# Decoder layer on Trainium2: the first weight slice in two quarters, and VectorE makes the first memory slice's high part

## What is computed

```python
h = rmsnorm(x, norm_g)
z = h @ w_in                                   # 2048 x 7168
...
mem_h = rmsnorm(mem, mem_norm_g)
mk, mv = jnp.split(mem_h @ w_mem_kv, 2, axis=-1)   # 2048 x 1024: keys, values
y_m = memory_attention(q_m, mk, mv) * jax.nn.silu(g_m)
...
y = jnp.concatenate([y_a, y_p, y_m], axis=-1) @ w_out
return rmsnorm(x + y, final_norm_g)
```

## Time and profile before

| what | us |
|---|---|
| median of 3 runs | 440.05 (439.99 to 440.51) |
| the profiled execution, its own time | 439.82 |
| span of its instructions | 437.6 |
| TensorE busy | 428.5 |
| VectorE busy | 266.3 |
| ScalarE busy | 220.1 |

### The profile page before, as it was taken

The page is one execution under the profiler, slowest core; times in us unless marked ns, Lnnn a source line. Parts: engine busy times, 40 slices in busy tenths (PEclk is TensorE's granted clock), DMA queues, the critical chain, the costliest instruction groups (busy, mean ns, idle before and its releaser), DMA issues.

```text
span 437.6 us, 6006 instructions
## 1 busy us (share of the span) xinstructions
PE 428.5 (98%) x2252; PEld 367.8 (84%) x2252; DVE 266.3 (61%) x293; ACT 220.1 (50%) x298; POOL 26.5 (6%) x48
## 2 busy tenths in 40 slices
PE   9999999999999999999999999999999999999992
PEld 8888888888888888888988888888888888888881
DVE  4865865545464685746466767848663674648522
ACT  6854784743444435536545444454465544357311
POOL 1000000000000020000020200010000202020200
PEclk9999999999999999999999999999999999999998
DMA  8999969655556554643629866445735256746022
GB/s 286 405 402 411 389 197 381 193 187 183 190 176 193 188 169 161 189 145 99 194 97 355 318 202 199 160 168 185 219 119 192 95 175 212 228 156 194 0 97 97
DMA packets 25657, 89.77 MB, mean 205 GB/s; under 512 B 2976, under 2 KB 3232, under 8 KB 24736
## 3 DMA queue, kind: packets, MB, share of 16 engines
q1 hardware_dynamic: 24336, 81.69, 54.9%
q10 hardware_dynamic: 1296, 7.73, 4.3%
HBM read 87.31 MB, written 2.10 MB: 204 GB/s over the span
## 4 chain that ended last, share of the span: by engine, by line
PE 95%; issue 2%; DVE 0%; POOL 0%; ACT 0%; POOLq 0%; DVEq 0%
PE ps L365 38%; PE ps L368 17%; PE ps L387 11%; PE ps L389 11%; PE ps L388 11%; PE ps L374 1%; PE ps L444 1%; PE ps L404 1%; PE ps L435 1%; PE ps L431 1%; PE ps L399 1%; PE ps L419 1%; PE ps L403 0%; PE ps L436 0%; PE ps L415 0%
## 5 line engine op out<-in xcount | busy, mean ns | idle before, releaser
L699 DVE TENSOR_TENSOR w_lo<-w_raw,w_hi 128x1024 fp32r<-128x1024 f32 x137 | 173.9, 1282 | 119.4 <-ACT w_hi L524 119.0
L524 ACT ACTIVATE w_hi<-w_raw 128x1024 fp32r<-128x1024 f32 x137 | 143.7, 1058 | 130.1 <-PE ps L368 74.6
L365 PE MATMUL ps<-xT,w_hi 128*128 128x512 f32 x640 | 200.6, 397 | 0.0
L368 PEld LDWEIGHTS ps<-xT,w_lo 128*128 128x128 f32 x600 | 112.7, 188 | 26.6
L368 PE MATMUL ps<-xT,w_lo 128*128 128x256 f32 x600 | 118.1, 278 | 0.0
L365 PEld LDWEIGHTS ps<-xT,w_hi 128*128 128x128 f32 x640 | 98.8, 189 | 1.3
L387 PE MATMUL ps<-w_hi,yT 128*128 128x512 f32 x112 | 43.6, 389 | 0.0
L388 PE MATMUL ps<-w_lo,yT 128*128 128x512 f32 x112 | 43.6, 389 | 0.0
L389 PE MATMUL ps<-w_hi,yT 128*128 128x512 f32 x112 | 43.6, 389 | 0.0
L387 PE MATMUL ps<-w_hi,xT 128*128 128x512 f32 x64 | 25.5, 399 | 0.0
L389 PE MATMUL ps<-w_hi,xT 128*128 128x512 f32 x64 | 25.0, 390 | 0.0
(11 more groups left out here) (129 smaller groups left out, 384.9 us busy)
## 6 DMA issues: line engine op xcount, KB each, us to landing
w_raw<-in_w_in SPq DMA_DIRECT2D x96, 512.0 KB, 4.2
w_raw<-in_w_out SPq DMA_DIRECT2D x32, 512.0 KB, 4.2
w_raw<-in_w_mem_kv SPq DMA_DIRECT2D x13, 512.0 KB, 13.1
x_t_raw<-in_x_t SPq DMA_DIRECT2D x8, 256.0 KB, 13.6
rows<-in_x ACTq DMA_DIRECT2D x2, 1024.0 KB, 10.5
rows<-in_mem ACTq DMA_DIRECT2D x2, 1024.0 KB, 9.0
x_res<-in_x ACTq DMA_DIRECT2D x2, 1024.0 KB, 8.9
mem_raw<-in_mem_head SPq DMA_DIRECT2D x3, 512.0 KB, 7.6
```

The costliest lines, as they stand in the source:

```text
L365: pe.matmul(ps[:, bank0(g) + f, :], hi[:, t, f * P:(f + 1) * P], moving[:, kt], start=(kt == 0), stop=(kt == KT - 1), skip_group_check=True)
L368: m = pe.matmul(ps[:, bank0(g) + f, 0:S], lo[:, t, f * P:(f + 1) * P], moving[:, kt, 0], start=False, stop=(kt == KT - 1), skip_group_chec ...
L524: act.activation(halves_of(n)[0], w_raw[:, n % RAW], ACT.Copy).then_inc(hi_done, 1)
L699: dve.tensor_tensor(lo, w_raw[:, n % RAW], hi.bitcast(F32), ALU.subtract).then_inc(lo_done, 1)
```

## The change

ScalarE issues weight slice (0, t=0) as two DMAs of 256 columns each (two quarters of a piece) and makes the high part of each quarter when it has landed. VectorE, not ScalarE, makes the high part of memory slice 0, as soon as the slice has landed; its waits for the table and for the constants stand behind its work on the first three pieces. TensorE runs 8 products of ones instead of 10. A new function `first_slice` does the t = 0 half of piece 0 in twelve matmuls of 256 columns: high x high (two features after each quarter), then high weights x low memory slice, then low weights x high memory slice.

```diff
+        quarter_landed = [sem(f"quarter_landed{i}") for i in range(2)]
+        quarter_hi = sem("quarter_hi")
+        mem_first_hi = sem("mem_first_hi")
...
+            def first_slice():
+
+                hi, lo = halves_of(0)
+                for f in range(NF):
+                    if f % 2 == 0:
+                        pe.wait_ge(quarter_hi, f // 2 + 1)
+                    pe.matmul(ps[:, bank0(MK) + f, 0:S], hi[:, 0, f * P:(f + 1) * P], memT[:, 0, 0],
+                              start=True, stop=False, skip_group_check=True)
+                pe.wait_ge(mem_lo, 1)
+                for f in range(NF):
+                    pe.matmul(ps[:, bank0(MK) + f, S:], hi[:, 0, f * P:(f + 1) * P], memT[:, 0, 1],
+                              start=False, stop=False, skip_group_check=True)
+                pe.wait_ge(first_lo, 1)
+                for f in range(NF):
+                    pe.matmul(ps[:, bank0(MK) + f, 0:S], lo[:, 0, f * P:(f + 1) * P], memT[:, 0, 0],
+                              start=False, stop=False, skip_group_check=True)
...
-                for t in range(TPP):
+                for t in range(int(n == 0), TPP):
...
-                    if n == 0 and t == 0:
-                        pe.wait_ge(first_lo, 1)
...
-            keep_warm(10, 7)
+            keep_warm(8, 7)
+            pe.wait_ge(mem_first_hi, 1)
+            first_slice()
...
-                    pe.wait_ge(mem_lo, TPP * (a + 1) if a >= HALVED else TPP * a + 1)
+                    if n:
+                        pe.wait_ge(mem_lo, TPP * (a + 1) if a >= HALVED else TPP * a + 1)
...
-                if n == 0:
-                    pe.wait_ge(first_hi, 1)
-                elif n < HALVED:
+                if 0 < n < HALVED:
                     pe.wait_ge(first_lo, n + 1)
...
-                if t == 0:
+                if n == 0 and t == 0:
+                    for q in range(2):
+                        c = slice(q * COLS // 2, (q + 1) * COLS // 2)
+                        act.wait_ge(quarter_landed[q], 16)
+                        act.activation(w_hi[:, 0, 0, c], w_raw[:, 0, 0, c], ACT.Copy).then_inc(quarter_hi, 1)
+                elif t == 0:
...
-            act.dma_start(w_raw[:, 0, 0], kv_dram[0, 0, :, 0]).then_inc(first_landed[0], 16)
+            for q in range(2):
+                c = slice(q * COLS // 2, (q + 1) * COLS // 2)
+                act.dma_start(w_raw[:, 0, 0, c], kv_dram[0, 0, :, 0, c]).then_inc(quarter_landed[q], 16)
...
-                    mem_to_hi((TPP * n + t,))
+                    if n or t:
+                        mem_to_hi((TPP * n + t,))
...
-                    dve.wait_ge(first_hi, n + 1)
+                    if n == 0:
+                        dve.wait_ge(quarter_hi, 2)
+                    else:
+                        dve.wait_ge(first_hi, n)
...
-                    dve.wait_ge(mem_hi, kt + 1)
+                    if kt:
+                        dve.wait_ge(mem_hi, kt)
+                    else:
+                        dve.wait_ge(mem_first_hi, 1)
...
-            dve.wait_ge(table_loaded, 1)
-            dve.wait_ge(consts_ready, 3)
+            dve.wait_ge(mem_first_landed, 16)
+            dve.tensor_scalar(memT[:, 0, 0], mem_t(0), mem_raw[:, 0:1], None, ALU.mult).then_inc(mem_first_hi, 1)
...
+            dve.wait_ge(table_loaded, 1)
+            dve.wait_ge(consts_ready, 3)
```

More of the change, by code:

```diff
@@ L467, in _ @@
                     pe.wait_ge(y_lo, min(a // 2 + 1, len(GATES)))
-                if n == 0:
-                    pe.wait_ge(first_hi, 1)
-                elif n < HALVED:
+                if 0 < n < HALVED:
                     pe.wait_ge(first_lo, n + 1)
-                else:
+                elif n:
                     pe.wait_ge(lo_done, n + 1)
@@ L544, in mem_to_hi @@
                 for kt in kts:
-                    if kt == 0:
+                    if kt == 1:
                         act.wait_ge(mem_first_landed, 16)
-                    elif kt in MEM_CHUNKS:
+                    if kt in MEM_CHUNKS:
                         act.wait_ge(mem_landed[MEM_CHUNKS.index(kt)], 16)
```

## The result

The changed kernel takes 442.69 us (median of 6, 441.0 to 443.48) against 440.05: **slower by 0.54%**, ratio 1.0054, 95% interval 1.0044 to 1.0064 (the two medians themselves stand 0.60% apart). The forecast was 440.4 in a range up to 441.3. The profiled execution took 441.66, with a span of 439.6, 2.0 us more than before. Note the spread: 2.5 us over six executions, where the kernel before has 0.5.

The account below looks back on a forecast made before the run. TensorE's unbroken stream behind piece 4, gated by a DMA landing, was taken as the bound. A second half 0.8 us late, less 0.41 absorbed, gave piece 4 0.4 us later: 440.4 us for the median, range 439.5 to 441.3.

Parts of the forecast that it names:

- The head start: Start of piece 0: fewer warm-up matmuls, VectorE's scaling and quarter copies let TensorE start at about 4.57, 0.76 us sooner.
- What the split moves in the queue: ScalarE's DMA queue: 128 more packets ahead put memory slice 1 back from 5.42 to at most 6.45, taken as about 6.25.
- nothing is paid: ScalarE's start: one DMA more takes 0.45 us and pushes the table load, which ends before anything has landed.
- The second half: Piece 0, t = 1: 1.76 us from slice landing to low weights, start at 8.1, 0.8 us late, at most 0.95.
- the point of 1.29 us: Delay and clock together beyond which the kernel counts as slower: 0.41 us of pauses plus 0.88 us of measuring tolerance.
- The absorption of 0.41 us: Ahead of pieces 3 and 4: TensorE's pauses of 0.18 and 0.23 us vanish and take up that much delay.
- piece 4's gate: Start of piece 4: the chain from its weights' DMA landing stays at 17.49, since the bytes ahead are the same.
- The clock: Rival, early TensorE work: new pauses make the clock rise later, costing 1.0 to 1.5 us more, 441.4 to 441.9; chance 0.17.
- the two rivals: Start of the kernel: clock rising later, chance 0.17, and memory slice landing later still, about 441.1, chance 0.06.
- Absorbed whole: Rival, first DMA queues: bytes set the pace, quarters and slice land as early as before, 440.0 us; chance 0.24.
- my two readings of the turns: DMA queues: turns by packet count whatever the size put the slice at up to 6.45; by bytes it stays at 5.42.

Follow-up runs that it names:

- late_wait: Kernel before, with ScalarE waiting for GpSimd's masks between its two DMAs, so memory slice 1 is issued at 2.05 us: 441.09 us, ratio 1.0032.
- tiny_third: Kernel before, with one extra DMA of a single 80-byte run on ScalarE's queue ahead of memory slice 1: 441.07 us, ratio 1.0034.
- sp_holds_back: late_wait, with SyncE's third DMA (memory slices 2 and 3) also held back, to 2.73 us: 441.34 us, ratio 1.0030 to the kernel before.
- split_only: Kernel before, with only the first weight slice's DMA split into two of 256 columns; ScalarE waits for both, then copies the whole: 441.58 us, ratio 1.0036.
- fill_pauses: Changed kernel, with products of ones put into TensorE's three pauses (ten instead of eight at the start, one, two): 441.60 us, ratio 1.0033 to the kernel before.
- one_dma: Changed kernel, with the first weight slice brought by one DMA again and the rest of the change kept: 440.25 us, ratio 1.0004 to the kernel before.
- split_by_rows: Kernel before, with the first weight slice in two DMAs of 64 partitions each, runs staying 2 KB: 442.14 us, ratio 1.0058.
- after_again: The changed kernel measured once more, nothing altered: 442.91 us, ratio 1.0057 to the kernel before.
- ten_warm: Changed kernel, with ten products of ones instead of eight ahead of the first slice: 441.74 us, ratio 1.0040 to the kernel before.
- slice_second: Changed kernel, with memory slice 1's DMA issued between the two quarters instead of behind them: 443.30 us, ratio 1.0074 to the kernel before.

## Why the prediction was wrong, step by step

- **The head start**: two products fewer, VectorE's scaling (0.35 us forecast, 0.35 measured) and a quarter's copy (0.39 and 0.42) were right. TensorE started at 5.2, not 4.57, because in this execution the first landings came at 4.48 and 4.66, not 4.14; the second quarter's copy started at 5.71, not 5.2. It made no difference, since the first slice ended before the second half could start.
- **What the split moves in the queue** is the step that failed. "Then 128 packets more in front of the memory slice put it back by 128/124 = 1.03 us, from 5.42 to at most 6.45." It was put back by 1.76 us, to 7.18. I counted packets within ScalarE's queue, at the rate of 124 a microsecond from an undisturbed stretch, and left out what the later issue of the slice does; the queue then passed 89 from 4 to 5 us and 89 from 5 to 6. late_wait has no packets more in front of the slice and makes it as late (7.50), and tiny_third nearly so (6.90); sp_holds_back, with SyncE's third transfer held back, takes the delay away (5.86). So the later issue, which lets SyncE issue a 256 KB transfer ahead of the slice or beside it, delays the slice by itself. I had noted the extra 0.45 us of issue and costed it only for the table load ("nothing is paid"), not for the DMA behind it.
- **The second half**: from landing to start 1.76 us forecast with 0.1 on top, 1.87 measured. Right; the error came in with its starting point: 1.74 us late instead of 0.8, outside my bound of 0.95. That alone crosses the point of 1.29 us that the prediction gave.
- **The absorption of 0.41 us** at pieces 3 and 4: right, both pauses are gone. The ground that I gave for piece 4's gate, that it stays because the bytes in front of it are the same, does not hold: its weights' copy starts at 14.90 in the changed kernel and up to 15.79 in the others (split_only), instead of 14.37. In the changed kernel TensorE is later still, so it cost nothing there.
- **The clock** was a rival at 0.17 and came true as a second term, on top of the first: 0.7 us in one trace, 2.2 in the other, 1.1 between the medians of the changed kernel and fill_pauses. The row that the Trainium skill's rule was set beside, an unbroken start, was the right place to look: by "TensorE: Matmul & The Clock Gate", "What's actually happening", activity releases the clock, and with the pauses filled the full level was there by 6.1 us. The pause ahead of the second half came from the late landing, and with the slice on time no such loss is seen (one_dma), so the two rivals were one chain, which I had priced as if apart.
- **"Absorbed whole"**, the reading that I tied to the Trainium skill's "DMA: Bandwidth & Descriptors" (turns by packets of bundled descriptors), did not come about; neither of my two readings of the turns fits split_by_rows.
- The forecast 440.4 and the chance of 0.73 for no change were wrong; slower had 0.22.

What stays open: the bytes ahead explain 256 KB, about 0.8 us at the 0.32 MB a microsecond of the earlier trace rows, of the 1.76. How much of the rest is the second quarter in front and how much the later issue was not separated. In the kernels of the table above the DMA engines were also less busy between 5 and 6 us (0.64 to 0.83, against 0.93 in the kernel before), but not in after_again (0.94), whose slice was late, and they were in sp_holds_back (0.80), whose slice was not; why they idle with transfers issued was not settled. Why one execution's clock rises at 10.4 and another's at 13.8, and why it falls behind one pause and not behind a longer one, was not either.

## What to carry to other kernels

While the first transfers are in flight, splitting one is not free: here each DMA issue took its engine some 0.45 us, and what stood behind it lost its place to what the other engine issued meanwhile. Cost the issue time of a DMA at the transfer behind it, for both queues together, and the stream behind it too: moving the DMA to the other queue cost 0.14 to 0.19% still. And a pause early in TensorE's work is to be priced together with the clock: here the level cost 0.7 and 2.2 us on top of the delay.

## What was not expected of the hardware

- ScalarE's 128 KB, issued at 1.2 us, took 3.5 to 4.5 us to land, and issued at 1.68 it took 5.3 to 6.0. In the changed kernel 0.49 us of later issue went with 1.76 us of later landing. Issued at 2.05 it took 5.4 with SyncE's third transfer issued before it (late_wait) and 3.8 with that one held back (sp_holds_back).
- A DMA of 80 bytes ahead of a transfer delayed its landing by 1.2 to 1.5 us.
- The printed granted clock stayed at 1.00 in stretches where matmul spacings show 1.2 GHz (to 10.4 and to 13.8 us in two executions of one kernel). In every trace where it fell to 0.50 (ten_warm, split_only, late_wait, slice_second), matmuls at the full spacing had come before.
- A DMA written behind a table load on ScalarE was issued while the table was loading, at 1.25 us.
